# Attention blocks in the order differential, chunk, MLA, with the value projection and the MLA up-projections issued between them

## The reference

```python
def first_block(x, positions, ...):
    for l in range(2):
        proj = rms_norm(x, attn_norm[l]) @ w_in[l]
        h_mla, h_diff, h_ch = split(proj)
        # 6 heads. q = rms_norm(c_q) @ w_uq (64 plain + 32 rotated columns a head),
        # k_nope, v = rms_norm(c_kv) @ w_ukv, k_rope shared by the heads; causal by chunks of 64
        o_mla = rms_norm(mla_attention(h_mla, ...), mla_out_norm[l])
        # 6 heads of two maps: p = softmax(map 0) - lam * softmax(map 1), distance bias
        o_diff = diff_attention(h_diff, ...)
        # 4 heads, a relative bias, chunks of 64, nothing masked within reach but the future
        o_ch = rms_norm(chunk_attention(h_ch, ...), chunk_out_norm[l])
        x = x + concat(o_mla, o_diff, o_ch) @ w_out[l]
        x = x + conv_ffn(rms_norm(x, ffn_norm[l]), ...)
    return rms_norm(x, final_norm)
```

## Time and profile before

| | |
|---|---|
| median of three executions | 2249.31 us (2247.08 to 2257.26) |
| profiled execution | 2237.74 us |
| its span, from the first to the last recorded instruction | 2236.0 us |
| mean granted TensorE clock | 0.965 |
| PE busy | 2055.1 us, 92% of the span |
| DVE / ACT / POOL busy | 1187.9 / 692.9 / 743.4 us |
| share of PE in the chain that ended last | 78% |

### The profile page before, as it was taken

One profiled execution on the slowest core, in us unless ns is written; L12 is line 12 of the kernel. 1 busy time (PEld: TensorE's weight loads), 2 busy tenths in 40 slices (PEclk: granted clock), 3 DMA queues, 4 the chain that ended last, 5 costly groups with the idle time before them and its releaser, 6 DMA issues.

```text
span 2236.0 us, 24957 instructions
## 1 busy us (share of the span) xinstructions
PE 2055.1 (92%) x8468; PEld 1325.8 (59%) x8469; DVE 1187.9 (53%) x1968; ACT 692.9 (31%) x1230; POOL 743.4 (33%) x1218
## 2 busy tenths in 40 slices
PE   7999889999998999889999999999998897987885
PEld 5865468888786874367888786454333445333332
DVE  6546766678546446777678644236872524111113
ACT  4328734334323217834334322120001501101010
POOL 0306766756201006776666300004660001111110
PEclk9999999999999999999999999999999997999998
DMA  4210022232233210022333222122331133799984
GB/s 172 85 41 1 39 94 104 104 113 98 87 103 112 94 50 1 38 85 94 104 104 115 85 92 94 64 88 94 113 113 57 79 147 155 320 423 423 424 319 156
DMA packets 44259, 284.19 MB, mean 127 GB/s; under 512 B 8394, under 2 KB 8650, under 8 KB 21632
## 3 DMA queue, kind: packets, MB, share of 16 engines
q1 hardware_dynamic: 34272, 254.35, 30.2%
q0 software_dynamic: 9024, 19.08, 2.2%
q10 hardware_dynamic: 864, 9.44, 1.0%
HBM read 272.68 MB, written 23.60 MB: 133 GB/s over the span
## 4 chain that ended last, share of the span: by engine, by line
PE 78%; DVE 8%; DMA 7%; ACT 3%; POOL 2%; issue 2%; SPq 0%; DVEq 0%; POOLq 0%; ACTq 0%
PE bank L808 11%; PE bank L810 10%; PE bank L809 10%; DMA experts<-in_experts 6%; PE bank L1058 5%; PE bank L1232 4%; PE bank L992 3%; PE bank L993 3%; PE bank L994 3%; PE bank L1028 2%; PE bank L1163 2%; PE bank L928 2%; PE bank L899 2%; PE bank L1235 2%; PE bank L915 1%
## 5 line engine op out<-in xcount | busy, mean ns | idle before, releaser
L808 PE MATMUL bank<-h_high,w_high 128*128 128x512 f32 x1056 | 418.0, 396 | 39.3 <-ACT h_high L1597 13.7
L809 PE MATMUL bank<-h_low,w_high 128*128 128x512 f32 x1056 | 414.9, 393 | 0.0
L810 PE MATMUL bank<-h_high,w_low 128*128 128x512 f32 x1056 | 414.8, 393 | 0.0
L1465 ACT ACTIVATE w_high<-extra 128x2048 fp32r<-128x2048 f32 (+1 forms) x104 | 180.6, 1737 | 347.3 <-DVE w_low L1868 347.2
L1865 DVE TENSOR_SCALAR extra<-ring 128x2048 int32<-128x2048 int32 (+1 forms) x104 | 116.9, 1124 | 262.7 <-PE bank L810 137.6
L808 PEld LDWEIGHTS bank<-h_high,w_high 128*128 128x128 f32 x1056 | 201.0, 190 | 92.0 <-issue 27.3
L810 PEld LDWEIGHTS bank<-h_high,w_low 128*128 128x128 f32 x1056 | 200.6, 190 | 42.7
L809 PEld LDWEIGHTS bank<-h_low,w_high 128*128 128x128 f32 x1056 | 201.2, 190 | 41.3
L1868 DVE TENSOR_TENSOR w_low<-ring,extra 128x2048 fp32r<-128x2048 f32 (+1 forms) x104 | 217.3, 2090 | 3.6
L1232 PE MATMUL bank<-experts,rstd 128*64 128x512 f32 x512 | 129.2, 663 | 29.2 <-DMA experts<-in_experts 28.5
L993 PE MATMUL bank<-act_low,w_high 128*128 128x512 f32 x352 | 139.0, 395 | 0.0
(11 more groups left out here) (434 smaller groups left out, 3691.7 us busy)
## 6 DMA issues: line engine op xcount, KB each, us to landing
experts<-in_experts SPq DMA_DIRECT2D x34, 2048.0 KB, 24.1
ring<-in_w_ffn_in SPq DMA_DIRECT2D x44, 1024.0 KB, 4.8
experts<-in_experts SPq DMA_DIRECT2D x34, 1024.0 KB, 21.8
ring<-in_w_ffn_out SPq DMA_DIRECT2D x32, 704.0 KB, 4.0
ring<-in_w_feature SPq DMA_DIRECT2D x14, 1024.0 KB, 4.8
ring<-in_w_rest SPq DMA_DIRECT2D x9, 1024.0 KB, 4.9
ring<-in_w_out SPq DMA_DIRECT2D x8, 1024.0 KB, 4.9
powers_d<-work POOLq DMA_DIRECT2D x16, 512.0 KB, 3.1
```

The lines of the kernel that those rows point to most:

```text
L808: pe.matmul(dst, high[:, at], h_high[:, k, :], start=k == 0, stop=False)
L809: pe.matmul(dst, high[:, at], h_low[:, k, :], start=False, stop=False)
L810: return pe.matmul(dst, low[:, at], h_high[:, k, :], start=False, stop=k == KD - 1)
L1465: act.activation(w_high[par_][:, 0:words], w_part[par_][:, 0:words], ACT.Copy).then_inc(w_split, 1)
```

## The change

- The order of the attention blocks is differential (t = 0 to 23), chunk (24 to 39), MLA (40 to 63).
- The 12 token tiles are issued by PE within the attention steps, one at each of t = -1 to 10, in banks 5 and 6. The 12 uq and uk tiles follow, alternating, at t = 13, 15, ... 35, and the four uv tiles at 37, 39, 41, 43, all in bank 6. The table `BETWEEN` holds the places; `up_tile` issues a small tile, `up_copy` is ACT's copy of it, `up_evac` DVE's work on it.
- A small tile waits for the copy of the one before, since they share a bank. Value products of all pairs use bank 5.
- ACT's two weight splits for the token blocks stand at t = 1 and 5 of its loop, the logarithms and exponentials of the MLA norms at t = 2; DVE's two at t = 0 and 4, and the normalisation of `cqkv` at t = 5.
- PBUF is 14: the block buffers lie in places free at that time, and the copy to `pt` uses the two halves of `x` instead of the ring. `x` is therefore stored to DRAM at the start of the second layer (2 MB) and loaded back in both layers, after the value products of the last pair but one; the first residual add waits for it (`x_home`). The relative bias is loaded after the last token tile, and three of w_out's four weight blocks may load as soon as the ring is free.
- POOL builds MLA's mask at block 36, and starts its power table after the last turn. out_norm, its tiles and the first operand order of w_out follow the new order of pairs.

```diff
-MAPS = ([("mla", h, 0, i) for h in range(MLA_H) for i in range(NQ)]
-        + [("diff", 2 * h + s, m, i) for h in range(DIFF_H // 2) for i in range(NQ) for s in range(2) for m in range(2)]
-        + [("chunk", 2 * h + s, 0, i) for h in range(CH_H // 2) for i in range(NQ) for s in range(2)])
+MAPS = ([("diff", 2 * h + s, m, i) for h in range(DIFF_H // 2) for i in range(NQ) for s in range(2) for m in range(2)]
+        + [("chunk", 2 * h + s, 0, i) for h in range(CH_H // 2) for i in range(NQ) for s in range(2)]
+        + [("mla", h, 0, i) for h in range(MLA_H) for i in range(NQ)])
+TILE_OF_PAIR = (3, 4, 5, 6, 7, 0, 1, 2)
...
-PBUF = EXTRA_PROBS + 2
+PBUF = 14
...
+SMALL = [(name, h) for h in range(MLA_H) for name in ("uq", "uk")] + [("uv", tc) for tc in range(NQ)]
+BETWEEN = {n - 1: ("token", n // NQ, n % NQ) for n in range(TOKEN_BLOCKS * NQ)}
+BETWEEN.update({13 + 2 * n: name for n, name in enumerate(SMALL)})
...
-        ahead = t | 1 if t < NPB and PBLOCKS[t][0] != "mla" else t
+        ahead = t | 1 if t < FIRST_MLA else t
...
-        pt = [ring[n].rearrange("p (c t) -> p c t", c=NQ) for n in (1, 2)]
+        pt = [x[:, NQ * n:NQ * (n + 1), :] for n in range(2)]
...
-        probs = [extra[:, (6 + n) * T:(7 + n) * T] for n in range(EXTRA_PROBS)] + [cqkv[:, 1, :], cqkv[:, 2, :]]
+        probs = [spare[:, n, :] for n in range(CH_H)] + [v[:] for v in cmix]
+        probs += [rt[:, 4 * n:4 * n + 4].rearrange("p a c e -> p (a c e)") for n in range(2)] + [rstd[:, 1, :]]
+        probs += [work[:, (41 + n) * T:(42 + n) * T] for n in range(3)] + tmp[2:4]
...
                 if l:
-                    sp.wait_ge(pe_done, done(l - 1, "ffn_out", KD - 1))
-                sp.dma_start(rel[:], a["rel"][l]).then_inc(rel_in, 16)
+                    sp.wait_ge(x_added, l * (2 * KD))
+                    sp.dma_start(x_d, x[:]).then_inc(x_parked, 16)
                 for n in range(RING, FEATURE_BLOCKS):
...
+                for n in range(RING):
+                    load(l, BLOCK_OUT + n, a["w_out"][l * BLOCKS_OUT + n])
+                sp.wait_ge(pe_done, done(l, "heads", PAIRS - 2, NQ - 1))
+                sp.dma_start(x[:], x_d if l else a["x"]).then_inc(x_home, 16)
+                for n in range(RING, BLOCKS_OUT):
                     load(l, BLOCK_OUT + n, a["w_out"][l * BLOCKS_OUT + n])
 
                 for n in range(RING):
...
+                def up_tile(name, n):
+                    if name == "uq":
+                        w = weights(l, BLOCK_MLA)
+                        pe.wait_ge(token_out, l * (4 * NQ) + TOKEN_BLOCKS * NQ)
+                        pe.wait_ge(mla_normed, l * 3 + 3)
+                        pe.wait_ge(uq_out, l * (2 * MLA_H) + 2 * n)
+                        for k in range(2):
+                            ins = pe.matmul(bank[6][:], w[:, (k * MLA_H + n) * P:(k * MLA_H + n + 1) * P], cqkv[:, k, :],
+                                            start=k == 0, stop=k == 1)
+                    elif name == "uk":
+                        w = weights(l, BLOCK_MLA + 1)
+                        pe.wait_ge(uq_out, l * (2 * MLA_H) + 2 * n + 1)
+                        ins = pe.matmul(bank[6][0:NOPE, :], w[:, n * NOPE:(n + 1) * NOPE], cqkv[:, 2, :], start=True, stop=True)
...
+                        w = weights(l, BLOCK_MLA + 1)
+                        pe.wait_ge(uq_out, l * (2 * MLA_H) + 2 * MLA_H)
+                        pe.wait_ge(token_out, l * (4 * NQ) + TOKEN_BLOCKS * NQ + n)
+                        ins = pe.matmul(bank[6][:, 0:MLA_H * MLA_V], cqkv[:, 2, n * P:(n + 1) * P],
+                                        w[:, MLA_H * NOPE:MLA_H * (NOPE + MLA_V)], start=True, stop=True)
+                    finish(ins, name, n)
...
+                        if kind == "mla" and i == 0:
...
+                            pe.wait_ge(uq_out, l * (2 * MLA_H) + 2 * (hd + 1))
+                            pe.wait_ge(roped, l * (MLA_H + 2) + (hd + 3))
...
-                        o = bank[5 + n % 2]
+                        o = bank[5]
...
+                            if n:
+                                pe.wait_ge(head_out, l * PAIRS + n)
...
+                    if t == FIRST_MLA - 4:
+                        pool.wait_ge(pe_done, done(l, "uq", MLA_H - 1))
...
+                pool.wait_ge(pe_done, done(l, "turn", NPB - 1))
...
+                def up_copy(name, n):
+                    act.wait_ge(pe_done, done(l, name, n))
+                    if name == "uq":
                         act.wait_ge(roped, l * (MLA_H + 2) + (n + 3))
-                        act.activation(qm[0:NOPE, n, :], bank[n % 4][0:NOPE, :], ACT.Copy, scale=MLA_SCALE).then_inc(uq_out, 1)
+                        act.activation(qm[0:NOPE, n, :], bank[6][0:NOPE, :], ACT.Copy, scale=MLA_SCALE).then_inc(uq_out, 1)
                     else:
...
+                    if t == 0 and l:
+                        act.wait_ge(x_parked, 16 * l)
...
+                    if t == 1:
+                        split_high(FEATURE_BLOCKS + 1, (FEATURE_BLOCKS + 1) % 2)
+                    elif t == 2:
+                        mla_roots()
+                    elif t == 5:
+                        split_high(BLOCKS_PROJ - 1, (BLOCKS_PROJ - 1) % 2, block_words(BLOCKS_PROJ - 1))
+                    elif t - 1 in BETWEEN and BETWEEN[t - 1][0] in ("uq", "uk"):
+                        up_copy(*BETWEEN[t - 1])
+                    if kind == "diff" and t % 2 == 0:
                         continue
                     while copied < t - LAG + (3 if kind == "diff" else 2):
                         turn(copied)
                         copied += 1
...
+                def up_evac(name, n):
+                    dve.wait_ge(pe_done, done(l, name, n))
+                    if name == "uq":
+                        rope(bank[6], qm[64:96, n, :], MLA_SCALE, n + 1).then_inc(roped, 1)
+                    else:
+                        dve.tensor_copy(vm[:, n, :], bank[6][:, 0:MLA_H * MLA_V]).then_inc(token_out, 1)
...
+                    if u == 0 and l:
+                        dve.wait_ge(powers_out, l * (ST // LAYERS) * 16)
+                    if u == PBUF - 2:
+                        dve.wait_ge(mla_normed, l * 3 + 3)
+                    if u == PBLOCKS[FIRST_CHUNK][3][0]:
+                        dve.wait_ge(rel_in, l * 16 + 16)
+                    if u == PBLOCKS[FIRST_MLA][3][0]:
                         dve.wait_ge(mask_made, 2 * l + 2)
...
+                    if t - 1 in BETWEEN:
+                        name, n, *rest = BETWEEN[t - 1]
+                        if name == "token":
+                            token_evac(n, *rest)
+                        elif name != "uk":
+                            up_evac(name, n)
+                    if t == 0:
+                        split_proj(FEATURE_BLOCKS + 1)
+                    elif t == 4:
+                        split_proj(BLOCKS_PROJ - 1)
+                    elif t == 5:
+                        normalise_cqkv()
                     if kind == "diff" and t % 2 == 0:
                         continue
                     first = t - 1 if kind == "diff" else t
```

212 lines of the change are left out of this document (99 added, 113 removed).

## The result

The changed kernel took 2262.55 us, the median of 16 executions (2257.18 to 2268.48), against 2248.49 us for the kernel before (16 executions on the same chip, 2239.76 to 2257.59). The ratio is 1.0058, with a 95% interval of 1.0043 to 1.0073: slower by 14 us. The forecast was 2277 us, 28 us slower: right in its sign, twice too large in its size.

The account below looks back on a forecast made before the run. PE was taken as the bound. Per layer -9.6 (tokens), -22.3 (small-tile stage gone), +29.1 (steps 12 to 37) and +11.8 (end) gave +9.0; two layers +18, clock +10, on the 2249.3 us median: 2277 us, range 2238 to 2303.

Parts of the forecast that it names:

- What bounds it: Whole kernel: PE, busy 92% of the span; the differential part is set by the round PE, DVE, ACT, POOL, PE.
- the token tiles: Steps -1 to 11: tokens among the first 12 differential blocks take 41.9 us instead of 51.5, a gain of 9.6 a layer.
- The waits: Steps 12 to 37: PE idles ahead of small tiles for ACT's copy of the one before, eleven waits, 21.75 us a layer.
- The clock: PE's clock falls to half at three or four of the 12 gaps in a layer's attention, costing 5 us a layer.
- The sum: Attention of both layers: +18 without the clock and +10 for it, +28 on the profiled execution's 2237.7 us, giving 2265.7.
- The step that failed: Last step, whole kernel: the median stands 11.6 us above the profiled execution, so 2249.3 + 28 = 2277 us.
- the term of +10: Attention of both layers: falls of PE's clock at 5 us a layer, +10 us in all.
- A term at nothing: Block buffers of the attention loop: two more can only loosen a wait, costed at 0 us.
- MLA at its steady pace: MLA blocks, moved from the start of attention: 28.4 us for 23 blocks instead of 23.9, 4.5 more a layer.
- hidden: Rival, small tiles: the bank comes back before PE asks, so no waits; 2221 us, chance 0.13.
- halved: Rival, small tiles: about 1 us of wait a tile and no fall of the clock; 2244 us, chance 0.17.
- `x` came home: Load of `x` ahead of the first residual add: hidden, costed at nothing; up to 10 us a layer without its cover.

Follow-up runs that it names:

- parking_only: Kernel before, with only the store of `x` to DRAM and its load back added: 2236.31 us, ratio 0.9965; its profiled execution took 2250.79 us.
- before_again: Kernel before, unchanged, profiled a second time: 2245.66 us, ratio 1.000.
- copy_mid: Changed kernel with, at the small tile's own step, DVE's rope behind the mixes and ACT's copy between two copies of turned blocks: 2220.40 us, ratio 0.9902.
- order_only: Changed kernel with token and small tiles ahead of the attention blocks, small tiles in four banks; order, 14 buffers and parking kept: 2236.90 us, ratio 0.9969.
- before_fourteen: Kernel before with 14 block buffers instead of 12, nothing else changed: 2226.25 us, ratio 0.9900.
- tokens_first: Changed kernel with the 12 token tiles in one piece ahead of the attention blocks, small tiles still between them: 2288.11 us, ratio 1.0203.

## Why the prediction was right and wrong

**What bounds it, and the token tiles: right.** Steps up to 11 took 40.5 us (forecast 41.9), PE full. Undoing this part alone cost 25.5 us in the medians and 19.4 in attention, against 19.2 forecast for two layers.

**The waits: right in place and size, in cause only in part.** 22.1 us a layer for 21.75, ahead of L890 and L895, ended by L1551 and L1553. What the text missed is the second path: it put the waits in the differential part down to ACT's list alone and gave the rope to the chunk part only. The waits ahead of a uq (14.7 us of 44.2) are as it says. Ahead of a uk (29.5), in both parts, the rope ended last in eleven of twelve cases, but only by 0.7 us on average. So the number came out right by the luck of two nearly equal paths, and the cure that it suggests (shorten ACT's) did not work alone.

**The clock: right against the profiled execution, not against the usual one.** 20.5 us a layer at 0.50, in five or six stretches where three or four were taken. From the layers of parking_only, (162.1 - 148.0) / 47.8 = 0.29 us are lost for each us at the lower level, so 6 us a layer; the profiled execution of before had 1 of them already, which leaves the 5 forecast. In executions like before_again, with 24 us in both layers, before had 3.5 a layer, which leaves 2.5. The Trainium skill, page "TensorE: Matmul & The Clock Gate", section "A second HAM failure mode: psum-queue depth-cycling", says that short idles repeated between groups of matmuls make the clock swing. The traces agree in part: with the waits cut to 13.7 us in all, copy_mid's first layer has no time at 0.50, and its second 3.4 us. But order_only, with nothing between its blocks, has 37.6 us, and parking_only 47.8 in one layer and none in the other, so these idles are not all that decides.

**The sum met the profiled executions.** It gave 2265.7 us; the changed kernel's took 2262.9 and 2266.0. A layer's attention was to grow from 149.6 by 9 + 5 to 163.6 us, and took 163.1 and 163.0. The stages bear it out: steps 12 to 39 sum to some 75 us without the clock (69.6, then a wait of 1.55, two uv tiles and steps 38 and 39), and took 82.9, 6 of it by the clock. No row was given for the 0.11 us of a change from one kind of matmul to another, 5.5 us of this sum, and no run measured it by itself.

**The step that failed** is the last: "The median is 11.6 us above that execution, so 2249.3 + 28". It took that distance for something that every kernel has. It is not: the changed kernel's median (2262.6) is that of its profiled execution (2262.9). The profiled execution of before was one with few falls of the clock. Its attention is at 0.50 for 6.8 us in the two layers, and for 24 us in before_again, whose attention is 6.2 us longer and whose other stages are 2 us longer; the changed kernel has its 41 us in both profiles. So most of that distance is clock that the changed kernel pays anyway: its falls were counted twice, once as the term of +10, reckoned from an execution with few, and once within the 11.6. Taken as it stands, 2265.7 would have been 3 us off. The last 3 of the 11.6 us are a matter of the set: in four others the median of before was 2245.6 to 2246.6, 8 to 9 above that execution.

**A term at nothing that is 20 us.** "Two more block buffers can only loosen a wait." They did, and the wait was there to see in the trace of before: a minimum that PE's turn releases. By parts, each run's median taken against before in its own set: 12 to 14 buffers -19.6 us; the new order with its parking and banks +10.9 (forecast +9, MLA at its steady pace); small tiles between the blocks +51.2 (forecast +38 with the clock); tokens between the blocks -28.5 (forecast -19.2). Such a chain of differences comes to the timed 14.1 by construction, so the total proves nothing; what the parts show is where the forecast was off. The profiles give the same chain for attention alone, in both layers: -13.1, +18.1, +41.4, -19.4, together +27.0 against the forecast's +28. So the 13 us that the buffers give stand against 9 more than forecast for the order and 3 more for the small tiles, in part by the clock (0 us at 0.50 in before_fourteen, 37.6 in order_only, 61 in tokens_first). The error in the buffers did not reach the total because the new stages were summed from PE's work and the waits, not from the old stages' times; but as a reading of the change it is wrong: the buffers, not the order, paid for much of what the small tiles cost.

**The rivals.** The waits were not hidden, nor halved, in the changed kernel. `x` came home 24 and 22 us early.

## What to carry to other kernels

An operation placed between two blocks costs not its own time but the longest path by which its buffer comes back: write out, for each engine, what stands ahead of the evacuation in its list, and move all of these together, since a path of equal length hides the cure of the other. Here a shift of the evacuations on ACT and DVE by a step turned 14 us of loss into 21 to 25 of gain. Most of that gain is to be had more cheaply: the kernel before with two more block buffers and nothing else gains 19.6, so the whole reordering at its best (copy_mid) is worth some 6 us beyond the buffers, at the uncertainty of two sets. Where a wait's releaser is the engine that frees a buffer (a minimum waiting for a turn), try a buffer more before moving any work. And compare a forecast made from a profiled execution with that execution, adding the distance to the median only where its cause is known.
